# A two-layer hybrid trunk on one core: TensorE takes the conditioning sums of an up step at the first tile of the next step instead of the fourth tile of the same step

## The reference: what is computed

```python
def conv_ffn(h, lp):
    up = depthwise_conv(h @ lp['ffn_up'], lp['ffn_dw'], lp['ffn_dw_b'])
    gate, val = up[..., :D_FF], up[..., D_FF:]
    return (jax.nn.silu(gate) * val) @ lp['ffn_down']

def trunk_layer(x, mod, lp, row, col, ctx):
    sh1, sc1, g1, sh2, sc2, g2 = jnp.split(mod[:, None, :], 6, axis=-1)
    h = rmsnorm(x, lp['pre_mix_g']) * (1.0 + sc1) + sh1
    mix, c_kv, k_pe = token_mixing(h, lp, row, col, ctx)
    x = x + g1 * rmsnorm(mix, lp['post_mix_g'])
    h = rmsnorm(x, lp['pre_ffn_g']) * (1.0 + sc2) + sh2
    x = x + g2 * rmsnorm(conv_ffn(h, lp), lp['post_ffn_g'])
    return x, c_kv, k_pe

    # per layer, for each of the two token groups
    mod = jax.nn.silu(c)[None, :] @ ada_w[l] + ada_b[l]
```

## Time and profile before

| | before |
|---|---|
| median of three runs | 2706.76 us |
| the profiled execution | 2703.79 us, span 2702.0 us |
| PE busy | 2463.7 us (91%) |
| DVE busy | 1661.1 us (61%) |
| POOL busy | 1310.3 us (48%) |
| ACT busy | 536.4 us (20%) |
| mean granted TensorE clock | 0.940 |

### The profile page before, as it was taken

The page is one execution under the profiler, slowest core; times in us unless marked ns, Lnnn a source line. Parts: engine busy times, 40 slices in busy tenths (PEclk is TensorE's granted clock), DMA queues, the critical chain, the costliest instruction groups (busy, mean ns, idle before and its releaser), DMA issues.

```text
span 2702.0 us, 44472 instructions
## 1 busy us (share of the span) xinstructions
PE 2463.7 (91%) x15092; PEld 2293.3 (85%) x15092; DVE 1661.1 (61%) x2288; ACT 536.4 (20%) x917; POOL 1310.3 (48%) x1232
## 2 busy tenths in 40 slices
PE   7897989999988999999969878899999699999996
PEld 7895548999978999999969744699999699999995
DVE  4558765554458776775464786545545687777655
ACT  1203432101012111112121134410111211111221
POOL 1458314555542555555525771165555165554552
PEclk9997989999987999999969989999999699998998
DMA  5220102333331322322213101133333132332221
GB/s 205 61 56 13 35 14 94 113 101 116 119 105 28 114 89 89 90 64 73 71 27 84 39 10 39 33 122 95 114 119 120 46 90 90 89 90 82 71 73 56
DMA packets 100492, 212.11 MB, mean 78 GB/s; under 512 B 10209, under 2 KB 17825, under 8 KB 100385
## 3 DMA queue, kind: packets, MB, share of 16 engines
q1 hardware_dynamic: 84832, 151.66, 19.7%
q10 hardware_dynamic: 15552, 59.02, 6.1%
HBM read 207.71 MB, written 2.93 MB: 78 GB/s over the span
## 4 chain that ended last, share of the span: by engine, by line
PE 70%; DVE 13%; DVEq 9%; ACT 3%; issue 3%; DMA 1%; ACTq 0%; SPq 0%
PE ps L503 41%; PE ps L853 11%; PE ps L523 4%; DVEq L1285 3%; DVE ada_part L1282 3%; PE ps L721 3%; PE ps L573 3%; PE ps L536 2%; DVEq L1693 2%; PE ps L667 1%; DVEq L1551 1%; PE ps L710 1%; PE ps L697 1%; DMA ada_pre<-in_w_ada_dram 1%; PE ps L587 1%
## 5 line engine op out<-in xcount | busy, mean ns | idle before, releaser
L443 POOL TENSOR_SCALAR w_hi<-w_raw 128x512 fp32r<-128x512 f32 x552 | 378.9, 686 | 1184.5 <-PE ps L503 306.9
L445 POOL TENSOR_TENSOR w_lo<-w_raw,w_hi 128x512 fp32r<-128x512 f32 x552 | 758.4, 1374 | 81.4 <-issue 1.1
L503 PE MATMUL ps<-h_hi,w_hi 128*128 128x322 f32 x2688 | 632.5, 317 | 0.0
L503 PE MATMUL ps<-h_lo,w_hi 128*128 128x322 f32 x2688 | 628.5, 316 | 0.0
L503 PE MATMUL ps<-h_hi,w_lo 128*128 128x322 f32 x2688 | 624.5, 314 | 0.0
L503 PEld LDWEIGHTS ps<-h_lo,w_hi 128*128 128x128 f32 x2688 | 463.5, 193 | 0.0
L503 PEld LDWEIGHTS ps<-h_hi,w_hi 128*128 128x128 f32 x2688 | 462.0, 193 | 1.3 <-issue 1.3
L503 PEld LDWEIGHTS ps<-h_hi,w_lo 128*128 128x128 f32 x2688 | 463.0, 192 | 0.0
L1282 DVE SCALAR_TENSOR_TENSOR ada_part<-ada_raw,cond,ada_part 128x384 f32<-128x384 f32 x448 | 346.4, 814 | 17.0
L1713 DVE TENSOR_TENSOR a_lo<-act,a_hi 128x644 fp32r<-128x644 f32 x88 | 136.4, 1554 | 145.9 <-ACT a_hi L1197 144.9
L1696 DVE SCALAR_TENSOR_TENSOR up_y<-up_x,par,up_y 128x644 f32<-128x644 f32 x176 | 188.1, 1109 | 11.6 <-issue 8.4
(11 more groups left out here) (208 smaller groups left out, 3391.0 us busy)
## 6 DMA issues: line engine op xcount, KB each, us to landing
w_raw<-in_w_lin_dram SPq DMA_DIRECT2D x360, 256.0 KB, 2.6
ada_raw<-in_w_ada_dram ACTq DMA_DIRECT2D x32, 1536.0 KB, 6.6
w_raw<-in_w_merge_dram SPq DMA_DIRECT2D x144, 256.0 KB, 2.7
ada_pre<-in_w_ada_dram ACTq DMA_DIRECT2D x4, 2048.0 KB, 23.0
w_raw<-in_w_merge_dram SPq DMA_DIRECT2D x48, 128.0 KB, 2.0
pw<-in_w_pair_dram SPq DMA_DIRECT2D x8, 640.0 KB, 4.0
x<-in_x_dram SPq DMA_DIRECT2D x8, 322.0 KB, 6.9
out_y_dram<-x SPq DMA_DIRECT2D x8, 322.0 KB, 2.3
```

Of the source, the lines that this page charges most:

```text
L443: pool.tensor_scalar(w_hi[:, s, 0:n * P], raw, 1.0, 0.0, ALU.mult, ALU.add)
L445: pool.tensor_tensor(w_lo[:, s, 0:n * P], raw, w_hi[:, s, 0:n * P], ALU.subtract).then_inc(w_split[s], 1)
L503: last = pe.matmul(ps[:, 2 * s + j, 0:HALF], w, a[:, j * HALF:(j + 1) * HALF], start=(k == 0 and i == 0), stop=(k == total - 1 and i == 2))
```

## The change

PE takes trios 4, 5, 6 and 7 ahead of tile 0 of steps 3, 5, 7 and 9 (before: ahead of tile 3 of steps 2, 4, 6 and 8), and trio 8 ahead of tile 1 of step 10 (before: ahead of tile 3 of step 9). ACT keeps the sums and starts the next load at the same, new places. DVE's sums stay where they are, but for trio 8, which moves from before the first half of step 9 to before the second half. No instruction is added or taken away.

```diff
-                def up_step(i, trio=None, ada_set=3):
+                def up_step(i, trio=None, ada_set=0):
                     for j in range(4):
                         pe.wait_ge(set_empty[j], set_use(L, "up", j, 1) + i)
                         if trio is not None and j == ada_set:
...
                 up_step(1, late_trio(L, 3), 0)
                 with pe.Fori(0, 3) as r:
-                    up_step(r * 2 + 2, late_trio(L, 4) + r)
-                    up_step(r * 2 + 3)
-                up_step(8, late_trio(L, 7))
-                up_step(9, late_trio(L, 8))
-                up_step(10)
+                    up_step(r * 2 + 2)
+                    up_step(r * 2 + 3, late_trio(L, 4) + r, 0)
+                up_step(8)
+                up_step(9, late_trio(L, 7), 0)
+                up_step(10, late_trio(L, 8), 1)
...
-                up_step(1, keep="rows", row=2 * ADA_TRIO, trio=2, ada_set=0)
+                up_step(1, keep="rows", row=2 * ADA_TRIO, trio=2)
                 with ac.Fori(0, 3) as r:
-                    up_step(r * 2 + 2, keep="rows", row=r * ADA_TRIO + 3 * ADA_TRIO, trio=r)
-                    up_step(r * 2 + 3)
-                up_step(8, keep="rows", row=6 * ADA_TRIO, trio=6)
-                up_step(9, keep="last")
-                up_step(FFC // 2 - 1, last=True)
+                    up_step(r * 2 + 2)
+                    up_step(r * 2 + 3, keep="rows", row=r * ADA_TRIO + 3 * ADA_TRIO, trio=r)
+                up_step(8)
+                up_step(9, keep="rows", row=6 * ADA_TRIO, trio=6)
+                up_step(FFC // 2 - 1, last=True, keep="last", ada_set=1)
...
-                def up_step(i, last_step=False, trio=None):
-                    if trio is not None:
-                        ada(trio)
+                def up_step(i, last_step=False, trio=None, before=0):
                     for q in range(2):
+                        if trio is not None and q == before:
+                            ada(trio)
...
                 up_step(8, trio=late_trio(L, 7))
-                up_step(9, trio=late_trio(L, 8))
+                up_step(9, trio=late_trio(L, 8), before=1)
                 up_step(FFC // 2 - 1, last_step=True)
```

More of the change, by code:

```diff
@@ L1152, in _, with up_step @@
                 next_h(L, "gap2", 1, SQ_GAP2, L * 2 + 1, L * NINV + 3, hx_up)
-                def up_step(i, first=False, last=False, keep=None, row=None, trio=None, ada_set=3):
+                def up_step(i, first=False, last=False, keep=None, row=None, trio=None, ada_set=0):
                     for j in range(4):
```

## The result

The changed kernel takes 2663.86 us (median of four runs, 2659.5 to 2667.02), against 2707.12 us before (median of four, 2701.76 to 2714.19). The ratio is 0.9827, 95% interval 0.981 to 0.9844: 1.7% faster. The profiled execution has a span of 2657.7 us, 44.3 less than before.

The account below looks back on a forecast made before the run. PE was taken as the bound, stopped and slowed in the up stage by DVE's late sums. Saving 6.0 us at eight places, 48 us, and 0 for trio 8 gave 2656, as a median 2659 us; range 2646 to 2680, own range 2650 to 2668.

Parts of the forecast that it names:

- What bounds, and what one wait costs: PE in the up stage: each late DVE sum costs 7.2 us: 3 idle, 1.2 sums, 3 low clock.
- nothing else: PE's up-stage waits: five on DVE's conditioning sum in each layer, 14.9 us in all, and no others.
- The move of trios 4 to 7: Up-stage loop: sum ready 4.1 us early, no idle or low clock; 6.0 us saved at eight places, 48 us.
- What else could hold PE: POOL's split of tile 2's second weight slot, wanted half a tile into the odd step: slack 1.4 us, cost nothing.
- DVE over a round: DVE's two-step round: 56 us of work against PE's 58.5, so it catches up with 2.5 us to spare.
- Four halves of 10.8: DVE's two-step round: four halves of 10.8 us each, with a sum of 12.6, are 56 us.
- The move of trio 8: Ahead of tile 1 of step 10: still 3 us idle plus low clock, 7.2 us as before; saving 0.
- The sum: Total saving of 48 us: 2656 us for a profiled execution, 2659 us for the median.
- Weights late: Rival: PE stops half a tile into odd steps if the chain takes over 1.4 us more; 2667 to 2691 us, chance 0.13.
- The clock does not come back: Rival: one-column sums between tiles lower the clock, so only 24 us are saved; 2683 us, chance 0.04.
- The tail sum gets cheaper: Rival: DVE finishes trio 8 some 3 us earlier, saving 6 more in both layers; 2647 us, chance 0.05.
- Longer sums: Rival: POOL, busier beside DVE, holds up the sum, 24.2 us instead of 12.6; 2743 us, chance 0.03.

Follow-up runs that it names:

- e3: Changed kernel's move for trios 4, 5 and 6 only, trios 7 and 8 placed as in the kernel before: median 2665.68 us, span 2666.6.
- e1: Kernel before, sums at their old places, DVE doing only four of the eight blocks of each up-stage trio: median 2641.89 us, span 2640.9.
- e7: Kernel before, sums at their old places, DVE doing seven of the eight blocks of each up-stage trio: median 2684.46 us, span 2684.4.
- e8: Kernel before, each up-stage sum of DVE given four more operations (first two done three times): median 2728.69 us, span 2726.4.
- e4: Changed kernel, each up-stage sum of DVE given four more operations (first two done three times): median 2672.92 us, span 2672.3.
- e6: Changed kernel, each up-stage sum of DVE given eight more operations (first two done five times): median 2693.66 us, span 2694.7.
- e10: e6 with ACT releasing tile 2's second weight slot ahead of the first half's tanh instead of behind it: median 2701.80 us, span 2696.3.
- e11: Changed kernel with ACT releasing tile 2's second weight slot ahead of the first half's tanh: median 2661.88 us, span 2655.7.
- e2: Changed kernel with trio 8 taken at the third tile of step 10 instead of the second, on PE and ACT: median 2651.67 us, span 2649.6.
- e9: e2 with trio 3 also taken at the second tile of step 1 instead of the first: median 2648.78 us, span 2643.5.

## Why the prediction was right

**Time.** 2659 was forecast, 2663.86 measured, in the range and in the forecast's own one.

**What bounds, and what one wait costs.** Right. 7.2 us a wait, 1.2 a sum in time: e3 gives 5.9 us by the spans and 6.8 by the medians for each moved sum where 6.0 stood, e1 shows that sums in time at the old place do the same, and the pieces of 57.35 us show the 1.24 us between them. 7.2 is a mean and not a price that each wait has: by the table under e7 and e8 the single waits of the kernel before cost 5.6 to 7.8 us, because the low clock behind them took 1.6 to 3.4. That the low clock is a part of its own and not just a share of the idle time e7 shows: with more than a third of the idle time taken away, four of ten stops still have 3.4 us of it, four 1.7 or 1.8 and two next to none. The prediction's "nothing else" is not quite so: its window left out a sixth wait on a sum, that of trio 3 at step 1 (1.78 and 1.51 us in the two layers). The change does not touch it.

**The move of trios 4 to 7.** Right: 58.6 us a round (58.5 forecast), no wait, clock 1.00.

**What else could hold PE.** Right in place and mechanism, and a little too generous in size: 1.4 us forecast, 1.15 in the profile after, and e4 shows a wait of 0.3 once the sum is 1.4 us longer. e6 and e10 show that it is this chain: the release alone moves the wait.

**DVE over a round.** "Four halves of 10.8" was wrong already for the kernel before, whose halves take 8.3, 9.6, 10.5 and 10.8 us; only the last had been read. After, they take 8.3, 12.1, 11.8 and 10.6. DVE's convolution (L1696) has a mean of 1233 ns after and 1109 before. POOL's pause speeds one half, and its backlog, which now falls on the next two, slows them; that the rows show side by side, and e11, with the pause cut short, has the one longer (8.4) and the next shorter (10.65). The round still closes with 2.9 us to spare. That 2.5 was forecast is luck: a half that was too long for the old kernel happened to be right for the new one.

**The move of trio 8.** The place was right, the size off: 3.0 us of idle time was forecast, 4.23 and 3.95 came. DVE starts the first half of step 9 at 1120.38, 0.9 us after the end of tile 1 as forecast, but takes 11.7 us for it instead of 10.8, while POOL works off its backlog, and the sum takes 12.9 instead of 12.6. From the start of the wait to the first down matmul it is 1170.87 - 1140.98 = 29.9 us, 8.4 beyond the three tiles, where 7.2 was assumed: 1.2 us in each layer.

**The sum.** 48 us forecast. The up stages gave 46.4: 2.4 less for trio 8, 1.6 more in the first layer, where by chance PE did not wait at step 1 this time, and the rest within the rounding. The span gave 44.3. The other 2.1 us lie in stages that the change does not touch: in the chains, from the first layer's third down chunk to the last tile of the second layer's out stage it is 874.0 us before and 875.1 after, and 875.8, 876.4, 876.5 and 877.4 in e4, e2, e3 and e1. The whole stretch from the first layer's third down chunk to the end of the second layer's step 0 (where PE comes to trio 3) takes 980.4 us in the kernel before, 981.5 in the changed one and up to 990.0 in e9. That looks like scatter between executions with the kernel before at its low end; I did not test it. It also means that a few microseconds of agreement between a forecast and a span prove little here; the readings inside the up stages carry the argument.

**The rivals.** "Weights late" did not happen, but was 1.15 us away. "The clock does not come back" is refuted by the windows above. "The tail sum gets cheaper" is refuted: it got dearer. "Longer sums": the sum stayed at 12.6 us in the changed kernel, but e10 shows that the mechanism is real, with 2.7 us more as soon as POOL works beside it. The Trainium skill, page "SBUF — State Buffer", section "Who interferes with whom", describes such a clash between a VectorE operation with two SBUF inputs and a GpSimd operation that reads SBUF; these traces agree in kind (9.71 and 12.44 us for the same fourteen operations).

## What to carry to other kernels

In an in-order queue that is the bound, place a wait for a slower helper where the helper is surely done, and compute that from the helper's own chain (here the end of a tile plus a half plus the sum, 24.5 us, against three or four tiles). Count a stop of the matmul engine by more than its idle time: here each cost about twice its idle time on the mean, until the clock was back. After moving it, look for the next link with the smallest slack, and don't expect a gain from freeing that link if the engine that it lets run shares something with the one that you wait for.

## What the runs showed of the hardware that was not expected

The same stop of PE does not always lower the clock. In e6, one round after another, the timeline of PE has these:

```profile
999.02 0.58 PE L503 MATMUL ps<-h_hi,w_hi 128*128 128x322 f32 x2 [1.80 <-POOL w_lo L445]
999.42 0.71 PE L503 MATMUL ps<-h_lo,w_hi 128*128 128x322 f32 x2
999.94 0.74 PE L503 MATMUL ps<-h_hi,w_lo 128*128 128x322 f32 x2
```

```profile
1061.14 0.57 PE L503 MATMUL ps<-h_hi,w_hi 128*128 128x322 f32 x2 [1.74 <-POOL w_lo L445]
1061.54 0.46 PE L503 MATMUL ps<-h_lo,w_hi 128*128 128x322 f32 x2
1061.84 0.46 PE L503 MATMUL ps<-h_hi,w_lo 128*128 128x322 f32 x2
```

Behind 1.80 us of idle time the pairs are 0.54 us apart and the clock of the next 5 us is 0.66; behind 1.74 us it is 1.00 and they are 0.30 apart. So with stops just below 2 us the length alone does not say whether one costs 1.8 us or 3.3. Stops in front of the sums lost the clock at shorter lengths still. In e10 the pairs are 0.54 us apart behind 1.30 us:

```profile
1116.67 1.47 PE L536 MATMUL ps<-const,ada_part 128*128 128x1 f32 x12 [1.30 <-DVE ada_part L1285]
...
1118.39 0.74 PE L503 MATMUL ps<-h_lo,w_hi 128*128 128x322 f32 x2
1118.93 0.74 PE L503 MATMUL ps<-h_hi,w_lo 128*128 128x322 f32 x2
```

and another stop there, of 0.90 us, cost 1.8 us of low clock as well, while one of 1.79 us in e7 cost about 0.1. I did not find what tells them apart.

Adding operations to DVE's sum lengthened it by less than their own time: four operations of some 0.6 us made it 1.4 us longer, eight 3.0. The same fourteen others took 11.51, 10.46 and 9.71 us with none, four and eight ahead of them. The likely reason is that they were pushed out of POOL's way; e10, where POOL works beside them and they take 12.44, speaks for it.
